# Output projection and FFN turned over, and part of the output sums started inside the sparse attention

## The chip, the cores and the metric

One Trainium2 chip, one of its cores. The metric is the device time of one execution in microseconds (us), the median over several executions. Engines by the profile's names: PE (TensorE), PEld (its weight loads), DVE (VectorE), ACT (ScalarE), POOL (GpSimd), SP (SyncE, which issues all DMAs here).

## The reference, cut to what matters

One layer: three groups of attention heads (gated DeltaNet, dilated, native sparse = NSA) give `mix`, and then

```python
mix = jnp.concatenate([o_dn, o_dil, o_nsa], axis=-1)        # (512, 2048)
x = x + jnp.einsum('bsm,md->bsd', mix, w_out[l])             # output projection, 2048 x 2048
h = rmsnorm(x, norm2_g[l])                                   # x / rms(x) * g
u = causal_dwconv(jnp.einsum('bsd,df->bsf', h, ffn_up[l]), ffn_conv[l])   # 2048 -> 2 x 5632, width 3
u_gate, u_val = jnp.split(u, 2, axis=-1)
x = x + jnp.einsum('bsf,fd->bsd', jax.nn.silu(u_gate) * u_val, ffn_down[l])
return rmsnorm(x, final_g)
```

512 tokens, width 2048 (16 tiles of 128), all in float32.

## The kernel before, in words

**Products.** Every large product of two float32 operands is made of three float32r products: each operand is split into a high part (rounded to float32r) and a low part (the rest), and hi x hi, hi x lo and lo x hi are summed in one PSUM bank. So each step is 3 matmuls of 128x512. The weights come as one long stream in DRAM, in units of 1 MB, a unit being 4 "quarters" of 128 x 512. SP loads a unit into `w_raw` (2 units; `load_unit` L147, which waits until the unit before the last is split), ACT copies each quarter to `w_hi` (`split_hi` L174), DVE subtracts to get `w_lo` (`split_lo` L183), both in a ring of 8 quarters. ACT may split a quarter once PE has used the one 8 before it; at a stage's start 4 quarters are ahead (`AHEAD`). `project` (L222) takes one of 16 steps of a tile with the weights stationary and `h_hi`/`h_lo` (the activations, features on partitions) moving: the result has features on partitions.

**Stages.** DeltaNet, dilated attention, NSA's K/V and compression, then NSA in three rounds `r` = 0, 1, 2 (last), each with two heads (groups g = 0, 1) and four `attend_pe`/`attend_dve`/`attend_act` sequences of 4 query blocks. In rounds 0 and 1 PE's gaps are filled with steps of the next round's q projections (`fill`, counts per block); in the last round there is no fill, and DVE and ACT use their gaps to split 14 of the 16 `mix` tiles (`mix_step`), which SP has loaded back from the DRAM scratch `mix_d` into `h_lo`. The last two heads' outputs are stored too (L1339) and loaded back at the start of the next stage.

**Output projection** (L1503 to L1568): here `h` is stationary and the weights move (L1529), so the result has tokens on partitions and can be added to `xs` (x by tokens, 4 MB, loaded at L1512 between the first two weight units of the stage). 4 column groups of 16 quarters, 12 matmuls to a quarter. **Norm** (`normalize`, L247 to L314): sum of squares and root by ACT, scaling by DVE (L290), 64 transposes on PE (L310), split by ACT (L278) and DVE (L300) into `h_hi`/`h_lo`.

**FFN.** 11 groups of 4 hidden tiles. `up_pe` makes 8 products of 16 steps (`project`, banks 0 to 3); ACT and DVE apply the convolution (L1640, L1664, L1666), SiLU (L1643), the product (L1671) and the split into `g_hi` (L1645) and `g_lo` (L1673). `down_pe` (L1624) has `g` stationary and the weights moving, 4 column groups of 4 quarters in banks 4 to 7, which DVE adds into `xs` (L1686). `g` has two slots, and PE does up(i+1) before down(i). The end: squares and scaling by rows on ACT, DVE and POOL (L1728, L1746, L1735, L1770, L1771), then four DMAs of 1 MB (L1696).

**Places.** By the order of the declarations, a partition's SBUF holds `h_hi` at 0 to 32 KB, `h_lo` to 64, `w_raw` to 80, `w_hi` to 96, `w_lo` to 112, constants and small tiles to about 125, `xs` to about 157, a gain row to about 165, and in the FFN `g_hi` to about 181 and `g_lo` to about 197.

A stage is an `nc.Block`: all engines meet at its end before the next begins.

## Time and profile before

| | us |
|---|---|
| median of 3 runs | 2756.88 |
| lowest and highest run | 2753.33, 2757.06 |
| the profiled execution | 2752.52 |
| its span, first to last instruction | 2750.4 |

The page gives busy time by engine and the granted PE clock by slices; the chain of waits in order of time says which engine the end depends on; the table of stretches gives busy time and clock by stage; the timeline gives start and duration of single instructions. A matmul's duration on the page includes the time in which the next one already runs, so the pace of PE is read from starts, or from a stretch divided by its count.

### The profile page before, as it was taken

The page shows a single profiled execution, that of the slowest core. Times are in us where ns is not written, and L with a number is a line of the kernel's source. Part 1 is how long each engine was busy: PE and PEld are TensorE (multiplying, and loading weights), DVE is VectorE, ACT ScalarE, POOL GpSimd, SP SyncE. Part 2 cuts the span into 40 slices and gives each one's busy share as a digit, 9 for nine tenths or more (in the row PEclk, how much of TensorE's full clock was granted, in tenths as well). Part 3 has the DMA queues.
Part 4 walks back from the last instruction along what each step waited for, and adds up shares of the span by engine and source line. Part 5 has one row for each costly group of instructions (what it writes and reads, how often), then busy time and mean ns, then how long its engine had stood idle before and what let it go on. Part 6 is the DMA issues. An engine that isn't in the chain of part 4 may idle for free.

```text
span 2750.4 us, 33487 instructions
## 1 busy us (share of the span) xinstructions
PE 2603.5 (95%) x11940; PEld 2108.6 (77%) x11940; DVE 1325.3 (48%) x2205; ACT 862.2 (31%) x1601; POOL 72.9 (3%) x54
## 2 busy tenths in 40 slices
PE   7899999989999877998999999999999999999997
PEld 5777877767887544886888888888888888888886
DVE  4776666633344554334444444444444444444444
ACT  4333332332224433224332322232323232322223
POOL 0111011100000000000000000000000000000002
PEclk9999999999999987998999999999999999999999
DMA  4311111131325112422223222222222222223222
GB/s 157 138 59 37 65 65 50 35 115 62 122 92 193 39 61 95 150 92 79 92 92 107 92 97 104 92 92 93 92 102 98 107 94 92 92 93 108 92 92 92
DMA packets 41621, 255.94 MB, mean 93 GB/s; under 512 B 5088, under 2 KB 5344, under 8 KB 13068
## 3 DMA queue, kind: packets, MB, share of 16 engines
q1 hardware_dynamic: 41484, 254.09, 25.8%
q8 instruction: 89, 1.46, 0.2%
q14 instruction: 48, 0.39, 0.0%
HBM read 245.65 MB, written 13.67 MB: 94 GB/s over the span
## 4 chain that ended last, share of the span: by engine, by line
PE 53%; DVE 0%; ACT 0%; issue 0%; DVEq 0%; ACTq 0%
PE bank L222 35%; PE bank L1624 18%; ACT fin_squares L1728 0%; DVE xs L1771 0%; DVE xs L1770 0%; DVE xs L1686 0%; DVEq L1589 0%; ACT fin_rs L1731 0%; ACT L1731 0%; DVE fin_rs L1765 0%; ACTq L1727 0%; DVEq L1750 0%
## 5 line engine op out<-in xcount | busy, mean ns | idle before, releaser
L222 PE MATMUL bank<-h_hi,w_hi 128*128 128x512 f32 x2272 | 919.2, 405 | 29.9 <-DVE w_lo L183 27.3
L222 PE MATMUL bank<-h_lo,w_hi 128*128 128x512 f32 x2272 | 889.8, 392 | 0.0
L222 PE MATMUL bank<-h_hi,w_lo 128*128 128x512 f32 x2272 | 889.5, 392 | 0.0
L183 DVE TENSOR_TENSOR w_lo<-w_raw,w_hi 128x512 fp32r<-128x512 f32 x840 | 555.1, 708 | 420.6 <-ACT w_hi L174 419.1
L174 ACT ACTIVATE w_hi<-w_raw 128x512 fp32r<-128x512 f32 x836 | 488.7, 624 | 721.0 <-PE bank L1624 311.4
L222 PEld LDWEIGHTS bank<-h_hi,w_hi 128*128 128x128 f32 x2272 | 430.0, 189 | 125.4 <-DVE w_lo L183 19.4
L222 PEld LDWEIGHTS bank<-h_lo,w_hi 128*128 128x128 f32 x2272 | 429.2, 189 | 91.9
L222 PEld LDWEIGHTS bank<-h_hi,w_lo 128*128 128x128 f32 x2272 | 430.1, 189 | 87.7 <-issue 4.4
L1624 PE MATMUL bank<-w_hi,g_hi 128*128 128x512 f32 x704 | 277.9, 395 | 0.0
L1624 PE MATMUL bank<-w_lo,g_hi 128*128 128x512 f32 x704 | 277.8, 395 | 0.0
L1624 PE MATMUL bank<-w_hi,g_lo 128*128 128x512 f32 x704 | 277.8, 395 | 0.0
L1686 DVE TENSOR_TENSOR xs<-xs,bank 128x512 f32<-128x512 f32 x176 | 120.9, 687 | 225.8 <-PE bank L1624 220.3
L1664 DVE SCALAR_TENSOR_TENSOR ffn_val<-bank,ffn_wg,ffn_val 128x511 f32<-128x511 f32 x44 | 33.0, 750 | 387.3 <-ACT ffn_val L1640 387.3
L1640 ACT ACTIVATE ffn_val<-bank,ffn_wg 128x512 f32<-128x512 f32 x44 | 30.3, 688 | 424.2 <-PE bank L222 424.2
L1624 PEld LDWEIGHTS bank<-w_hi,g_lo 128*128 128x128 f32 x704 | 132.7, 188 | 30.9
L1624 PEld LDWEIGHTS bank<-w_lo,g_hi 128*128 128x128 f32 x704 | 132.6, 188 | 31.0
L1624 PEld LDWEIGHTS bank<-w_hi,g_hi 128*128 128x128 f32 x704 | 132.6, 188 | 31.0
L1529 PE MATMUL bank<-w_hi,h_hi 128*128 128x512 f32 x256 | 100.3, 392 | 2.0 <-DVEq L1552 2.0
L1529 PE MATMUL bank<-w_lo,h_hi 128*128 128x512 f32 x256 | 100.1, 391 | 0.0
L1529 PE MATMUL bank<-w_hi,h_lo 128*128 128x512 f32 x256 | 100.1, 391 | 0.0
L1746 POOL TENSOR_TENSOR xs<-xs,gain_row 128x512 f32<-128x512 f32 x12 | 16.4, 1418 | 2200.3 <-ACT fin_squares L1728 2200.3
L755 ACT ACTIVATE dn_Y<-bank 128x512 f32<-128x512 f32 x36 | 21.6, 599 | 152.1 <-PE bank L636 152.1
(281 smaller groups left out, 1988.7 us busy)
## 6 DMA issues: line engine op xcount, KB each, us to landing
w_raw<-in_weights SPq DMA_DIRECT2D x209, 1024.0 KB, 4.8
bias_rows<-bias_row SPq DMA_DIRECT2D x10, 512.0 KB, 7.3
mix_scratch<-head_out SPq DMA_DIRECT2D x16, 256.0 KB
xs<-in_x SPq DMA_DIRECT2D x1, 4096.0 KB, 14.6
out<-xs SPq DMA_DIRECT2D x4, 1024.0 KB, 6.1
x_t<-in_x_t SPq DMA_DIRECT2D x3, 1024.0 KB, 11.3
nsa_tab<-bias_rows SPq DMA_DIRECT2D x6, 448.0 KB, 7.2
h_lo<-mix_scratch SPq DMA_DIRECT2D x1, 2560.0 KB, 9.9
```

What stands on the lines that cost most here:

```text
L174: nc.scalar.activation(w_hi[:, act_q.n % RING, :], raw_quarter(act_q), ACT.Copy)\
L183: nc.vector.tensor_tensor(w_lo[:, s, :], raw_quarter(dve_q), w_hi[:, s, :].bitcast(F32), ALU.subtract).then_inc(lo_done, 1)
L222: m = nc.tensor.matmul(PB[pb][:], a[:, s, k], b[:, kt, :], start=(kt == 0 and n == 0), stop=(kt == KT - 1 and n == 2))
L755: nc.scalar.activation(B["Y"][:], W[1][:], ACT.Copy).then_inc(y_a, 1)
L1529: m = nc.tensor.matmul(bank[4 * c + b][:], x[:, kt, b * P:(b + 1) * P], w[:, s, :], start=(kt == 0 and n == 0), stop=(kt == KT - 1 and n = ...
L1624: m = nc.tensor.matmul(W[b][:], x[:, slot, kt, b * P:(b + 1) * P], w[:, s, :], start=(kt == 0 and n == 0), stop=(kt == GT - 1 and n == 2))
L1640: nc.scalar.activation(dst[:], PB[2 * (j % 2) + v][:], ACT.Copy, scale=fwg[:, v, 2, j:j + 1])\
L1664: link(dve, nc.vector.scalar_tensor_tensor(dst[:, 1:SEQ], bk[:, 0:SEQ - 1], fwg[:, v, 1, j:j + 1], dst[:, 1:SEQ], ALU.mult, ALU.add))
L1686: nc.vector.tensor_tensor(dst, dst, W[b][:], ALU.add).then_inc(dn_free, 1)
L1746: nc.gpsimd.tensor_tensor(xs[:, b, cc], xs[:, b, cc], fg[:, cc], ALU.mult).then_inc(fin_g, 1)
```

## The change

- `project` takes its moving operand from a list of tiles on request. The output projection uses `project`: weights stationary, `h` moving, 16 tiles of output features in banks 0 to 3, weights streamed by columns. The FFN's `down_pe` has the weights stationary and `g` moving.
- `x1` (features on partitions, loaded in four DMAs of 1 MB at the start of the stage) takes the place of `xs`. The norm is no stage of its own: squares are summed over tiles in `ssq` (`square`, `add_square`) as the tiles come, the unnormed `x1 * g2` is split (`h2_high`, `h2_low`), a ones-matmul sums `ssq` over partitions, and every `up` result is multiplied by 1/rms (`r2`) on DVE on its way out of PSUM.
- Places: `g_hi`, `g_lo` lie in the first four tiles of `h_hi`, `h_lo`, in one slot. The first four tiles of the FFN's input lie in `near`, the former `w_raw`; from unit 78 (`FFN_UNIT`) the raw weights go to `w_raw_far`, behind `x1`.
- Order: up(i), down(i), with one slot of `g`.
- In NSA's last round 16 steps (48 matmuls; 8 steps of each of output tiles 0 and 1) fill PE's gaps (`WO_FILLS`); their 4 quarters are the ones already split ahead. SP loads one more unit, which ACT and DVE split at the round's end, before DVE's last two copies. The last two heads are split straight from `ob`; no store, no load.
- The end: squares per tile, `ssq`, ones-matmul, root, reciprocal of 128x512, 16 scalings on DVE, eight DMAs of 512 KB.

```diff
+FFN_UNIT = 4 * DN_H + 3 * DIL_H + 6 * NSA_G + 2 * 4 + NSA_H + KT
...
+        near_at = nc.sbuf_base
         w_raw = sb(ctx, "w_raw", [P, 2, 4 * QW])
+        near = nc.alloc_sbuf_tensor_at("near", [P, 2 * GT, SEQ], F32R, offset=near_at)
...
+            hi, lo = (h_hi[:, kt, :], h_lo[:, kt, :]) if tiles is None else tiles[kt]
+            for n, (a, b) in enumerate(((w_hi, hi), (w_lo, hi), (w_hi, lo))):
+                m = nc.tensor.matmul(PB[pb][:], a[:, s, k], b,
...
+        WO_PAIR = [(u, kt) for q in range(4) for u in range(2) for kt in range(4 * q, 4 * q + 4)]
...
+            WO_FILLS = (0, 0, 0, 0), (0, 0, 0, 2), (2, 2, 2, 2), (2, 2, 2, KT)
+            def wo_filler(pe):
+                steps = iter(WO_PAIR[:len(WO_PAIR) // 2])
+                def fill(n):
+                    for u, kt in islice(steps, n):
+                        pe.wait_ge(m_lo, kt + 1)
+                        project(pe, u, kt)
+                return fill
...
             def nsa_dve(dve, r, last):
-                left = [0 if last else 8]
+                left = [4 if last else 8]
...
                 if last:
                     for _ in range(TB):
                         mix_step(mix_lo, dve)
+                    sp_lo(8)
...
-                    load_units(sp, (Q_HEAD + 8 * min(r + 1, NSA_R - 1) + AHEAD + 3) // 4)
+                    load_units(sp, (Q_HEAD + 8 * min(r + 1, NSA_R - 1) + AHEAD + 3) // 4 + (r == NSA_R - 1))
...
+        def h2_high(act, d):
+            nc.scalar.activation(h2[d][0], x1[:, d, :], ACT.Copy, scale=g2[:, d:d + 1]).then_inc(h2_a, 1)
+        def h2_low(dve, d):
+            dve.wait_ge(h2_a, d + 1)
+            nc.vector.scalar_tensor_tensor(h2[d][1], x1[:, d, :], g2[:, d:d + 1], h2[d][0].bitcast(F32),
+                                           ALU.mult, ALU.subtract).then_inc(h2_v, 1)
+        def residual(dve, d):
+            dve.wait_ge(q_used, Q5 + (4 * (d + 1) if d else 7))
+            nc.vector.tensor_tensor(x1[:, d, :], x1[:, d, :], PB[d % 4][:], ALU.add).then_inc(wo_free, 1)
+            dve.wait_ge(wo_free, 4 + d + 1)
...
             def _(sp):
-                sp.wait_ge(stored, 16 * KT + STORED2)
-                for kt in MIX_LATE:
-                    load_mix(sp, [kt], m_in[2])
+                for c in range(CG):
+                    sp.dma_start(x1[:, 4 * c:4 * c + 4, :], t["x_t"][:, 4 * c:4 * c + 4, :]).then_inc(xr_in, 16)
+                sp.dma_start(g2[:], t["g2"]).then_inc(g2_in, 16)
+                sp.dma_start(fg[:], t["final_g"]).then_inc(g2_in, 16)
+                load_units(sp, FFN_UNIT)
                 load_unit(sp)
...
+                for u, kt in WO_PAIR[len(WO_PAIR) // 2:]:
+                    pe.wait_ge(m_lo, len(MIX_EARLY) if kt < MIX_LATE[0] else KT)
+                    project(pe, u, kt)
+                for d in range(2, KT):
+                    pe.wait_ge(wo_free, d + 1)
+                    for kt in range(KT):
+                        project(pe, d % 4, kt)
...
+                dve.wait_ge(xr_in, 64)
+                dve.wait_ge(g2_in, 32)
+                for d in range(KT):
+                    split_lo(dve, 4 if d else 0)
+                    if d < KT - 1:
+                        residual(dve, d)
+                        add_square(dve, d)
+                for d in range(H2A):
+                    h2_low(dve, d)
...
-            g_hi = sb(c7, "g_hi", [P, 2, GT, SEQ], F32R)
-            g_lo = sb(c7, "g_lo", [P, 2, GT, SEQ], F32R)
+            g_hi, g_lo = h_hi[:, 0:GT, :], h_lo[:, 0:GT, :]
...
-                            for n, (x, w) in enumerate(((g_hi, w_hi), (g_lo, w_hi), (g_hi, w_lo))):
-                                m = nc.tensor.matmul(W[b][:], x[:, slot, kt, b * P:(b + 1) * P], w[:, s, :],
+                            for n, (w, x) in enumerate(((w_hi, g_hi), (w_lo, g_hi), (w_hi, g_lo))):
+                                m = nc.tensor.matmul(W[b][:], w[:, s, b * P:(b + 1) * P], x[:, kt, :],
...
+                        nc.vector.tensor_tensor(us[v], PB[2 * (j % 2) + v][:], r2[:], ALU.mult).then_inc(up_free, 1)
...
+                        if last and (c or b):
+                            square_sum(dve, 4 * c + b - 1)
...
+                up_pe(pe, 0, True)
+                with repeat(pe, N_GROUP - 1, (pe_q, GQ, "ffn_pe quarters")) as i:
+                    down_pe(pe, i)
+                    up_pe(pe, i + 1)
+                down_pe(pe, N_GROUP - 1)
+                pe.wait_ge(fin_ss, KT)
+                pe.wait_ge(dn_free, 4 + 16 * N_GROUP)
+                nc.tensor.matmul(W[0][:], ones, ssq[:], start=True, stop=True).then_inc(fin_ps, 1)
...
+                residual(dve, KT - 1)
+                dve.sem_inc(up_free, 1)
+                for d in range(H2A, KT):
+                    h2_low(dve, d)
+                add_square(dve, KT - 1)
...
+                square_sum(dve, KT - 1)
+                dve.wait_ge(fin_root, 1)
+                nc.vector.reciprocal(r2[:], r2[:]).then_inc(fin_ok, 1)
+                dve.wait_ge(fin_ok, 1)
+                for d in range(KT):
+                    nc.vector.scalar_tensor_tensor(x1[:, d, :], x1[:, d, :], fg[:, d:d + 1], r2[:], ALU.mult, ALU.mult)\
+                        .then_inc(fin_v, 1)
```

## Rows read from the trace of the kernel before

**Rows 1.** The page: busy time and share; granted PE clock in 40 slices, tenths.

```profile
PE 2603.5 (95%) x11940; PEld 2108.6 (77%) x11940; DVE 1325.3 (48%) x2205; ACT 862.2 (31%) x1601; POOL 72.9 (3%) x54
...
PEclk9999999999999987998999999999999999999999
```

**Rows 2.** The chain of waits in order of time: start, duration, what.

```profile
1459.31 44.63 PE bank L1624 x192
1503.94 87.06 PE bank L222 x384
```

**Rows 3.** Stretches: length, busy PE, PEld, DVE, ACT, POOL, clock, DMA share, GB/s.

```profile
1048.30:1062.40 14.10, 9.16 (x27) 5.23 (x26) 8.56 (x20) 6.22 (x18) 0.00 (x0) 0.74 0.00 0
...
1082.90:1258.40 175.50, 175.46 (x768) 145.03 (x768) 53.47 (x81) 46.71 (x74) 0.00 (x0) 0.99 0.35 130
1258.40:1285.00 26.60, 14.20 (x66) 12.30 (x65) 22.41 (x39) 14.58 (x29) 0.00 (x0) 0.68 0.00 1
...
1503.60:1590.70 87.10, 87.10 (x386) 72.14 (x385) 36.08 (x60) 24.19 (x42) 0.00 (x0) 1.00 0.28 97
```

**Rows 4.** Timeline of PE, NSA rounds 1 and 2: start, duration, operation [idle before].

```profile
973.39 0.33 PE L972 MATMUL bank<-cst,nsa_lg 128*128 128x128 f32 x1 [1.18 <-DVE nsa_lg L1004]
...
983.07 2.32 PE L986 MATMUL bank<-nsa_PT,nsa_v 128*128 128x512 f32 x8
986.42 0.33 PE L972 MATMUL bank<-cst,nsa_lg 128*128 128x128 f32 x1 [1.02 <-DVE nsa_lg L1004]
...
1052.22 0.27 PE L972 MATMUL bank<-cst,nsa_lg 128*128 128x128 f32 x1
...
1066.10 0.27 PE L972 MATMUL bank<-cst,nsa_lg 128*128 128x128 f32 x1
...
1076.33 4.63 PE L986 MATMUL bank<-nsa_PT,nsa_v 128*128 128x512 f32 x8 [0.69 <-ACT nsa_PT L1023]
```

**Rows 5.** Timeline of PE where the output projection begins.

```profile
1082.94 0.79 PE L1529 MATMUL bank<-w_hi,h_hi 128*128 128x512 f32 x1 [1.98 <-DVEq L1552]
1083.53 0.63 PE L1529 MATMUL bank<-w_hi,h_lo 128*128 128x512 f32 x1
1083.96 0.63 PE L1529 MATMUL bank<-w_lo,h_hi 128*128 128x512 f32 x1
```

**Rows 6.** Timeline of DVE at the end of NSA's last round.

```profile
1081.00 0.69 DVE L1318 COPY head_out<-bank 128x512 f32<-128x512 f32 x1 [2.28 <-PE bank L986]
```

**Rows 7.** Timelines of SP and of ACT in the output projection's first 20 us.

```profile
1084.60 1.31 SPq L147 DMA_DIRECT2D w_raw<-in_weights  x1
1085.95 0.43 SPq L1512 DMA_DIRECT2D xs<-in_x  x1
...
1090.79 2.20 ACT L174 ACTIVATE w_hi<-w_raw 128x512 fp32r<-128x512 f32 x4 [1.91 <-DMA w_raw<-in_weights]
1103.19 2.20 ACT L174 ACTIVATE w_hi<-w_raw 128x512 fp32r<-128x512 f32 x4 [10.20 <-DMA w_raw<-in_weights]
```

**Rows 8.** Timeline of DVE in the norm.

```profile
1262.67 2.74 DVE L290 SCALAR_TENSOR_TENSOR n_y<-xs,n_rs,gain_row 128x512 f32<-128x512 f32 x4
```

**Rows 9.** Timeline of PE, a compression product (two f32 matmuls in two passes each).

```profile
892.83 1.98 PE L1211 MATMUL bank<-cmp_PT,v_cmp 31*128 31x512 f32 x4
```

**Rows 10.** Timelines of ACT and DVE after an FFN up product.

```profile
1591.03 0.69 ACT L1640 ACTIVATE ffn_val<-bank,ffn_wg 128x512 f32<-128x512 f32 x1 [9.68 <-PE bank L222]
...
1591.83 0.75 DVE L1664 SCALAR_TENSOR_TENSOR ffn_val<-bank,ffn_wg,ffn_val 128x511 f32<-128x511 f32 x1 [8.88 <-ACT ffn_val L1640]
...
1594.94 0.69 DVE L1673 TENSOR_TENSOR g_lo<-ffn_prod,g_hi 128x512 fp32r<-128x512 f32 x1 [0.70 <-ACT g_hi L1645]
```

**Rows 11.** Groups by line: count, busy us, mean ns, idle before.

```profile
L183 DVE TENSOR_TENSOR w_lo<-w_raw,w_hi 128x512 fp32r<-128x512 f32 x840 | 555.1, 708 | 420.6 <-ACT w_hi L174 419.1
L174 ACT ACTIVATE w_hi<-w_raw 128x512 fp32r<-128x512 f32 x836 | 488.7, 624 | 721.0 <-PE bank L1624 311.4
...
L791 DVE RECIPROCAL dn_A<-dn_A 128x512 f32<-128x512 f32 x6 | 20.1, 3353 | 3.3 <-ACT dn_A L740 3.0
```

**Rows 12.** Timelines of DVE, PE, ACT and SP at the end.

```profile
2731.67 3.06 DVE L1686 TENSOR_TENSOR xs<-xs,bank 128x512 f32<-128x512 f32 x4 [8.10 <-PE bank L1624]
2733.33 0.40 PE L1624 MATMUL bank<-w_lo,g_hi 128*128 128x512 f32 x1
2735.58 1.28 ACT L1731 ACT_TABLE_LOAD   x1
...
2738.64 3.91 SPq L1696 DMA_DIRECT2D out<-xs  x4
```

More of the change, by code:

```diff
@@ L1199, in nsa_pe @@
                     m.then_inc(c_s, 1)
-                fill(8)
+                fill(0 if last else 8)
                 for g in range(NSA_G):
@@ L1267, in nsa_dve @@
             def nsa_dve(dve, r, last):
-                left = [0 if last else 8]
+                left = [4 if last else 8]
                 def sp_lo(k):
@@ L1862, in down @@
             rows(ffn_down, g * GT * P, c)
-    up(0)
-    for g in range(1, N_GROUP):
+    for g in range(N_GROUP):
         up(g)
-        down(g - 1)
-    down(N_GROUP - 1)
+        down(g)
     return np.stack(units)
```

402 lines of the change are left out of this document (155 added, 247 removed).

## The prediction

> **What bounds the kernel now.** I read first the busy shares and the clock by slices, then the chain of waits in order of time, then the stretches by stage, and single instructions at the seams last. PE is busy 95% of the span, at full clock but for three slices in the attention [rows 1]. In the FFN the chain is PE alone: one piece of 384 up matmuls and one of 192 down matmuls, eleven times over, with nothing between them [rows 2]. So work taken from DVE or ACT there is worth nothing, and only three things can move the end: the pace of PE's matmuls, the places where PE stands idle, and the tail after its last matmul. The idle places that this change touches are the last NSA round, where PE is busy 9.16 us of 14.1 at a mean clock of 0.74, and the norm, a stretch of 26.6 us with 64 small transposes; the output projection between them is dense: 768 matmuls in 175.5 us [rows 3].
>
> All sums below are against the profiled execution: span 2750.4 us, device time 2752.5. The median of the runs shown, 2756.9, is 4.4 us above it, and I add the change to the median at the end.
>
> **Step 1, the pace of the down projection.** Up: 87.06 us / 384 = 226.7 ns a matmul. Down: 44.63 / 192 = 232.4 ns [rows 2]. The output projection of before has the very loop shape of down (activations stationary, weights moving, a bank for every three matmuls) and takes (175.5 - 1.4)/768 = 226.7 ns [rows 3], the 1.4 us being its slow start (step 3). So neither which operand is stationary nor the banks cost anything; what is left as different is the place of `g`, above 165 KB, while all operands of the other two lie below 112 KB. The change puts `g` below 48 KB and leaves every operand of every large product below 112 KB, `near` included. I take 226.7 for down: 2112 x 5.7 ns = **-12.0 us**, all of it on the chain. Bounds: 0, if the place isn't the cause, and -12. In the Trainium skill, "TensorE: Matmul & The Clock Gate", section "Back-to-back issue gap", a warm matmul of 512 columns takes 518 cycles, about 216 ns, and nothing is said of where in SBUF its operands lie. By that rule moving them gains nothing, which is rival A; the trace agrees with neither its figure nor its silence, as it has two paces for one shape.
>
> **Step 2, the norm.** Of the 26.6 us [rows 3] nothing stays. In its place:
> - The meeting at the stage's end. At the last such seam DVE's last instruction ended at 1081.69 [rows 6] and PE began at 1082.94 [rows 5], 1.25 us later. Now PE itself ends last and DVE is done; I take 0.9 us, bound 1.3.
> - The first up product needs `h2` tile by tile. Tiles 0 to 3 (`near`) are ready before, 12 matmuls = 2.7 us of cover. The others wait for the residual of tile 15 (0.7), ACT (0.7) and DVE (0.75), so tile 4 comes some 2.9 us after the end against PE's 0.9 + 2.7 = 3.6; from there DVE makes one per 0.66 us (four in 2.74, [rows 8]) and PE eats one per 0.68. No stall, with little to spare: 0, bound 3.
> - The ones-matmul in full float32: two passes of about 0.43 (four in 1.98 us, [rows 9]): 0.9 us.
> - DVE then adds the last square, copies the conv taps and splits quarter 5 of the FFN while PE wants it: 0.3, bound 2.
>
> The root and the 3.35 us reciprocal [rows 11] run beside two or more products of 10.9 us, for which banks are free. Sum -26.6 + 0.9 + 0.9 + 0.3 = **-24.5 us**, bounds -26 and -20.
>
> **Step 3, the last NSA round and the output projection.** The 48 matmuls put into the round take 10.9 us of PE time there. They fit: in round 1 an attend with 7 fill steps takes 986.42 - 973.39 = 13.0 us, in the last round without any 1066.10 - 1052.22 = 13.9 [rows 4]; the pace is DVE's. The last PV product ran at half clock, 4.63 us against 2.32 [rows 4]; with PE busier it may gain up to 2.3. But at the round's end DVE now splits 4 quarters (4 x 0.71 [rows 11] = 2.8 us) before its two copies, which before waited 2.28 us for PE [rows 6]. The one takes back most of the other: PE begins the next stage 0.5 us earlier, bounds 3 earlier and 3 later.
>
> There 720 matmuls are left, 163.2 us. A start at half clock costs 1.4 us as it does now (7 matmuls at 0.43 instead of 0.23 [rows 5]). The new thing is the queue on SP. Now a unit of weights is issued first, then the 4 MB of x, then the next unit. In the new order x goes first, all 4 MB, then two small loads, and behind them the unit with the quarters after the first eight. ACT began on the first unit 4.9 us after its issue ended (1084.60 + 1.31), and 4 + 1 MB more took till 1103.19, that is 2.48 us a MB [rows 7]. So from the stage's start at about 1081.9: 0.7 for the first issue, 4.9 + 4 x 2.48 = 14.8 for x and the unit, 1.0 for the small loads (0 to 4; the trace has nothing of their size behind a full queue), 0.62 + 0.71 [rows 11] to split the first quarter: 1099.7. Who waits for it: DVE and ACT, which also wait for x and the gains before they take any split of the stage, and PE, whose 48 prepared matmuls carry it to 1082.4 + 10.9 + 1.4 = 1094.7. PE stalls 5.0 us and pays about 1.4 more for the half clock after it. Sum 163.2 + 1.4 + 5.0 + 1.4 = 171.0 against 175.5: -4.5, with the start -**5.0 us**, bounds -12 (no stall) and +4.
>
> **Step 4, the FFN's order.** With one slot, down(i) needs the g of its own up(i). It takes its quarters in order, so the last hidden tile is wanted 3 x 12 x 0.227 = 8.2 us after up's end. The chain now runs from 1591.03 to 1595.63, 4.6 us [rows 10]; the product with `r2` puts one DVE operation of 0.7 and a wait before it: 5.4. Cover 8.2, so **0**. Behind this chain on DVE stand the splits of the next quarters, wanted 10.9 us after; 5.4 + 0.7 is in time. DVE gains 88 products of 0.7 us = 60 us in all, in stretches where it is more than half idle (36.1 busy in 87.1 [rows 3]). Loads, x twice before and twice now: 0.
>
> **Step 5, the tail.** Now it is 2750.4 - 2733.73 = 16.7 us [rows 12]. New, from PE's last end T: DVE must do adds and square sums in turn for the last four tiles, nine operations of some 0.75 (four adds with waits take 3.06 [rows 12]) from T-1.85: T+4.9. Ones-matmul at half clock, as PE is idle: 1.9, T+6.9. Root on ACT 0.7 (its table load, 1.28 [rows 12], fits beside the matmul): T+7.6. Reciprocal 3.35 [rows 11]: T+11.0. Sixteen scalings at 0.66 [rows 8]: T+21.7. The last 512 KB: I take 4.0 for issue, transfer and landing, under the 4.9 of a 1 MB load [rows 7], as DVE's pace of 1.33 us per 512 KB is no faster than the queue's 1.24; the meeting 0.4. T+26.1, **+9.4 us**, bounds +6 and +12. Nothing hides it.
>
> **Sum**: -12.0 - 24.5 - 5.0 + 0 + 9.4 = **-32.1 us**: 2720.4 in terms of the profiled execution, 2724.8 in terms of the median.
>
> **Rivals.**
> - **A, the pace of down stays.** The 5.7 ns come from something else than `g`'s place. For: no row shows one operand in two places. Against: the output projection, same shape, at 226.7. Sum -20.1: 2736.8.
> - **B, the x load costs more.** Smaller pieces or the gains' loads hold the queue, or the filled last round is slowed by its steps as well: 10 us more than step 3. For: the only stage in which PE has but 11 us of stock against 16 us of queue. Against: the 4 MB ran at full rate before. -22: 2735.
> - **C, the single slot of g turns the FFN into stop and go, slower than before.** Place: the fourth tile of each down. If DVE doesn't take up the chain at once at up's end, since splits stand before it in program order, all 11 seams stall. The kernel becomes slower once each stalls more than (32.1 + 5.5)/11 = 3.4 us, so when the chain takes over 11.6 us instead of 5.4; with nothing covered it would be 11 x 5.4 = 59 us, +27: 2784. Against: at up's end in the trace ACT takes the bank at once and DVE follows 0.1 us after ACT [rows 10], its splits done by then.
> - **D, PE's end moves but the tail and the x load eat it**: rival A with the upper bounds of steps 2, 3 and 5: -20.1 + 4.5 + 9.0 + 2.6 = -4.0: 2752.9. For: all four are independent of each other and open. Against: it needs all of them.
>
> **How the numbers follow.** Forecast (all steps within their bounds, down at 226.7) 64%; A 14%; B 14%; C 4%; D 4%. The likeliest is the forecast, 2724.8. The range runs to A and B on the upper side, 2741 with the bound of the tail, and on the lower side to no stall in step 3, 2714. Faster by over 0.2% (5.5 us, about what a measurement of this kernel can tell from no change): forecast, A, B and a quarter of D, 93%; within 0.2%: half of D, 2%; slower: C and the rest of D, 5%.
>
> **What would show it.** Right: in the chain of waits the down pieces of 192 are 43.5 us long, and no wait of PE on `h_lo`/`g_lo` stands between the pieces; between the output projection and the first up piece there are under 4 us; PE waits some 5 us on `w_lo`, whose chain goes back to a weights DMA, some 11 us into the output projection; the stretch after the last FFN matmul is 26 us. Wrong: down pieces of 44.6 us (A); a gap of PE in front of the fourth quarter of each down (C); a wait on x or the weights of 10 us and more (B); fill matmuls after which the attention's transposes come later than 14 us apart (step 3).

## The result and the profile after

| | before | after |
|---|---|---|
| median | 2755.15 us | 2722.11 us |
| lowest and highest run | 2753.33, 2757.06 | 2718.94, 2723.40 |
| the profiled execution, and its span | 2752.5, 2750.4 | 2723.4, 2721.6 |

The ratio of after to before is 0.9878, with a 95% interval of 0.9861 to 0.9895: 33.0 us less, where 32.1 less had been predicted (2724.8 us, range 2714 to 2741, from the 2756.9 us of the first three runs; the median of before is now one of four). The number was right. Of its reason for the faster down projection, the second largest term, that can't be said: the runs below show another cause than the one predicted.

The page of the kernel after, busy time of PE and DVE and the granted PE clock in 40 slices, to be laid beside [rows 1]:

```profile
PE 2581.6 (95%) x11880; PEld 2098.2 (77%) x11880; DVE 1398.9 (51%) x2313; ACT 859.5 (32%) x1578; POOL 55.7 (2%) x42
...
PEclk9999999999999997999999999999999999999998
```

PE has 60 instructions and 21.9 us of work less: the 64 small transposes of the norm are gone, four passes of ones-matmuls came. One low slice of the clock is left where there were three, and a new one stands at the very end. The chain of waits in order of time (start, duration, what), for [rows 2]:

```profile
1256.78 11.17 PE bank L231 x48
1267.95 0.86 PE bank L1575 x2
1268.81 76.19 PE bank L231 x336
1345.00 43.52 PE bank L1588 x192
1388.52 87.04 PE bank L231 x384
```

From the first FFN product on PE has no gap. Line 231 is `project`, 1575 the ones-matmul of the norm, 1588 the down projection: 43.52 us for 192 matmuls, 226.7 ns each, where [rows 2] has 44.63. Next the stretches by stage (length, busy PE, PEld, DVE, ACT, POOL with their counts, clock, DMA share, GB/s), for [rows 3]; in order they are the output projection, the first FFN product with its seam, a down and an up piece, the last down group, and what follows PE's last FFN product:

```profile
1085.80:1256.60 170.80, 168.06 (x720) 138.22 (x720) 61.25 (x97) 44.35 (x81) 0.00 (x0) 0.97 0.32 117
1256.60:1268.30 11.70, 11.52 (x51) 9.38 (x51) 10.65 (x22) 10.75 (x19) 0.00 (x0) 1.00 0.52 191
1345.00:1388.50 43.50, 43.50 (x194) 36.03 (x193) 23.28 (x36) 13.22 (x22) 0.00 (x0) 1.00 0.28 97
1388.50:1475.50 87.00, 87.00 (x386) 72.06 (x385) 40.40 (x67) 24.88 (x42) 0.00 (x0) 1.00 0.27 97
2650.60:2696.50 45.90, 44.88 (x192) 35.30 (x191) 27.48 (x43) 16.33 (x28) 0.00 (x0) 1.00 0.07 23
2696.50:2721.60 25.10, 2.08 (x2) 0.50 (x2) 18.00 (x23) 3.87 (x6) 0.00 (x0) 0.56 0.42 167
```

The timeline of PE at both ends of the last attention round (start, duration, operation, [idle before]): the round's first product, its last PV product, the output projection's first matmul, and the first one after its only stall, for [rows 4, 5]:

```profile
1016.26 0.97 PE L1157 MATMUL bank<-k_cmp,nsa_q 128*128 128x31 f32 x7
...
1079.77 2.42 PE L923 MATMUL bank<-nsa_PT,nsa_v 128*128 128x512 f32 x8 [0.69 <-ACT nsa_PT L960]
...
1085.85 0.77 PE L231 MATMUL bank<-h_hi,w_hi 128*128 128x512 f32 x1 [3.66 <-PEq L1096]
...
1102.19 0.76 PE L231 MATMUL bank<-h_hi,w_hi 128*128 128x512 f32 x1 [2.39 <-DVE w_lo L191]
```

And of the kernel before, the round's first product:

```profile
1011.34 0.85 PE L1197 MATMUL bank<-k_cmp,nsa_q 128*128 128x31 f32 x6
```

With these the spans can be laid side by side, 2750.4 against 2721.6, -28.8 us:

| stretch | before | after | difference | predicted |
|---|---|---|---|---|
| start to the last round's first product | 1011.3 | 1016.3 | +4.9 | 0 |
| from there to the output projection's first matmul | 71.6 | 69.6 | -2.0 (see below) | -0.5 |
| output projection | 175.5 | 170.3 | -5.2 | -4.5 |
| norm and seam | 26.6 | 1.5 | -25.1 | -24.5 |
| eleven down pieces at their pace | | | -12.2 | -12.0 |
| stalls in the last down group | 0 | 2.4 | +2.4 | 0 |
| after PE's last FFN product | 16.7 | 25.1 | +8.4 | +9.4 |

The first line isn't the change's. The code up to there is the same in all kernels of this study, but for the places of tiles in three of them, and in the profiled executions that stretch ended anywhere from 1009.7 to 1016.3 us. Part of it shows in the stretch 944 to 976 us, where attention products begin (kernel before, after, and e4_tail below, in this order): the clock is 0.89, 0.84 and 1.00 there.

```profile
944.00:976.00 32.00, 26.46 (x105) 16.68 (x104) 17.11 (x55) 11.84 (x40) 0.00 (x0) 0.89 0.22 82
```

```profile
944.00:976.00 32.00, 27.49 (x105) 17.56 (x104) 14.41 (x46) 12.15 (x36) 0.00 (x0) 0.84 0.21 82
```

```profile
944.00:976.00 32.00, 25.86 (x114) 16.96 (x113) 18.24 (x57) 13.61 (x43) 0.00 (x0) 1.00 0.22 82
```

The second line scatters too, over less: in the profiled executions of nine further kernels whose last round is that of the kernel after, it reads 69.6 (e9_unit_tail) to 71.0 us (e7_g_mid), so between -0.6 and -2.0 against the one execution of before. So single profiles are compared below by stages, and whole kernels by medians. Without that line the change is worth -33.7 us by its stages. (The 1.5 us of the norm are 0.63 between the last product of the output projection and the first of the FFN, and the 0.86 of the ones-matmul.)

### The profile page after: what moved, and what is told of

It reads as the page before. It is cut to its first block, busy times and chain, and to the rows that moved or that the text cites. A ratio compares the mean times of both kernels' runs of the same rounds, so it can differ in the third digit from the quotient of the medians.

```text
span 2721.6 us, 33363 instructions
## 1 busy us (share of the span) xinstructions
PE 2581.6 (95%) x11880; PEld 2098.2 (77%) x11880; DVE 1398.9 (51%) x2313; ACT 859.5 (32%) x1578; POOL 55.7 (2%) x42
## 4 chain that ended last, share of the span: by engine, by line
PE 53%; DVE 1%; ACT 0%; issue 0%; DVEq 0%; ACTq 0%
PE bank L231 35%; PE bank L1588 17%; DVE x_t L1737 0%; DVE head_out L1668 0%; ACT head_out L1711 0%; DVE rms_row L1734 0%; PE bank L1690 0%; DVE x_t L1660 0%; PE bank L1575 0%; ACT rms_row L1713 0%; DVEq L1550 0%; ACTq L1710 0%; DVEq L1717 0%
## 5 line engine op out<-in xcount | busy, mean ns | idle before, releaser
L231 PE MATMUL bank<-h_hi,w_hi 128*128 128x512 f32 x2176 | 887.5, 408 | 36.9 <-DVE w_lo L191 32.0
L231 PE MATMUL bank<-h_lo,w_hi 128*128 128x512 f32 x2176 | 855.4, 393 | 0.0
L231 PE MATMUL bank<-h_hi,w_lo 128*128 128x512 f32 x2176 | 854.9, 393 | 0.0
L182 ACT ACTIVATE w_hi<-w_raw_far 128x512 fp32r<-128x512 f32 x528 | 307.1, 624 | 439.4 <-PE bank L1588 274.8
L191 DVE TENSOR_TENSOR w_lo<-w_raw_far,w_hi 128x512 fp32r<-128x512 f32 x528 | 331.2, 687 | 123.8 <-ACT w_hi L182 122.5
L191 DVE TENSOR_TENSOR w_lo<-w_raw,w_hi 128x512 fp32r<-128x512 f32 x312 | 215.8, 735 | 202.8 <-ACT w_hi L182 202.5
L1588 PE MATMUL bank<-h_hi,w_hi 128*128 128x512 f32 x704 | 274.4, 390 | 1.0 <-DVE x_t L1660 1.0
L1588 PE MATMUL bank<-h_hi,w_lo 128*128 128x512 f32 x704 | 273.9, 389 | 0.0
L1588 PE MATMUL bank<-h_lo,w_hi 128*128 128x512 f32 x704 | 273.9, 389 | 0.0
L231 PE MATMUL bank<-near,w_hi 128*128 128x512 f32 x704 | 231.5, 390 | 0.5 <-DVEq L1717 0.5
L182 ACT ACTIVATE w_hi<-w_raw 128x512 fp32r<-128x512 f32 x308 | 176.8, 621 | 94.4 <-DMA w_raw<-in_weights 48.7
L231 PEld LDWEIGHTS bank<-near,w_hi 128*128 128x128 f32 x704 | 132.1, 188 | 28.4 <-DVEq L1717 0.9
L231 PE MATMUL bank<-near,w_lo 128*128 128x512 f32 x352 | 136.9, 389 | 0.0
```

The source lines that it names most:

```text
L182: nc.scalar.activation(w_hi[:, act_q.n % RING, :], raw_quarter(act_q), ACT.Copy)\
L191: nc.vector.tensor_tensor(w_lo[:, s, :], raw_quarter(dve_q), w_hi[:, s, :].bitcast(F32), ALU.subtract).then_inc(lo_done, 1)
L231: m = nc.tensor.matmul(PB[pb][:], a[:, s, k], b, start=(kt == 0 and n == 0), stop=(kt == KT - 1 and n == 2))
L1588: m = nc.tensor.matmul(W[b][:], w[:, s, b * P:(b + 1) * P], x[:, kt, :], start=(kt == 0 and n == 0), stop=(kt == GT - 1 and n == 2))
```

## Experiments

All are edits of the kernel after, and differences are against its 2722.11 us. The kernel before was measured beside each group of them and had medians of 2755.1 to 2757.0 us, so a difference of 2 us between medians of different groups says little.

### What makes the down projection faster

The first question was whether `g`'s place does it. In the built programs the first tile starts at 16.1 KB (byte 16512), so all addresses are some 16 KB above the places that stand ahead of the prediction: `g` was at 181.5 to 213.5 KB, and the operands of all fast products of the kernels before and after lie below 128.2 KB. e1_g_high puts `g` alone back up:

```diff
-            g_hi, g_lo = h_hi[:, 0:GT, :], h_lo[:, 0:GT, :]
+            g_hi, g_lo = (sb(c7, n, [P, GT, SEQ], F32R) for n in ("g_hi", "g_lo"))
```

> The changed kernel with g_hi and g_lo, and nothing else, put back at the upper end of SBUF (two tiles of 8 KB behind all others, at about 179 to 195 KB) in place of the first four tiles of h_hi and h_lo. Theory (the place of the moving operand sets PE's pace): the down pieces of 192 matmuls in the chain of waits go back from 43.5 to 44.6 us, 232.4 ns a matmul, up pieces stay at 87.0; 2112 x 5.7 ns = +12.0 us against the changed kernel. Rival (the pace of before came from g being the stationary operand there, or from its two slots): down stays at 43.5 and the time is that of the changed kernel within 2 us.

Measured 2734.94 us (2733.47 to 2737.33), +12.8, and in the chain of e1_g_high:

```profile
1387.39 87.07 PE bank L231 x384
1474.46 44.80 PE bank L1588 x192
```

Up stays, down takes 44.80 us, 233.3 ns a matmul. So it is where `g` lies, moving or stationary. e5_w_hi_far moves the other operand, in the FFN only, up:

```diff
+            hi_far.append(sb(c7, "w_hi_far", [P, RING, QW], F32R)[:])
...
+            wh = hi_of(pe_q.n)
-            for n, (a, b) in enumerate(((w_hi, hi), (w_lo, hi), (w_hi, lo))):
+            for n, (a, b) in enumerate(((wh, hi), (w_lo, hi), (wh, lo))):
```

> The changed kernel with the ring of w_hi, from the FFN's first quarters on, in a new tile at the upper end of SBUF (about 182 to 198 KB); w_lo and all moving operands stay low. So the stationary operand of two of every three matmuls of the FFN, up and down, lies high. Theory in its wide form (any matmul operand high in SBUF slows PE, as each of the three did when g lay there): the pace goes from 226.7 to 232.4 ns for two thirds or for all of the FFN's 6336 matmuls, +24 to +36 us. Theory in its narrow form (in the kernel before it was the weight load of g, hidden or not, that differed; or only the moving operand counts): no difference, up pieces 87.0 and down pieces 43.5 us.

Measured 2749.23 us (2744.68 to 2751.45), +27.1: 6336 matmuls by (231.1 - 226.7) ns are 27.9. Chain of e5_w_hi_far:

```profile
1388.56 88.75 PE bank L237 x384
1477.31 44.37 PE bank L1596 x192
```

So the stationary operand counts too, and in up as in down: the wide form of the theory. Up to here everything fits the predicted reason, "high is slow". e7_g_mid looks for the border, and takes one possible confusion away (the tiles' start within 64 bytes); e8_pad tests that one by itself; e11_border lays the ring of `w_hi` over the range next to 128 KB:

```diff
+        sb(c5, "pad_mid", [P, 8])
+        g_hi, g_lo = (sb(c5, n, [P, GT, SEQ], F32R) for n in ("g_hi", "g_lo"))
         x1 = sb(c5, "x1_t", [P, KT, SEQ])
```

> The changed kernel with g_hi and g_lo in front of x1 and not behind everything: by the allocator's addresses, which begin with the first tile at 16 KB, at 141.5 to 157.5 KB (in e1_g_high 189.6 to 205.6 KB, in the kernel before 181.5 to 213.5, the operands of all fast products below 128.2 KB). Start on a multiple of 64 bytes, as the tiles of the fast products have and those of e1_g_high and e5_w_hi_far had not. Theory (height: a border lies somewhere between 128 and 181 KB): either 43.5 or 44.6 us for a down piece, which tells on which side of 141.5 KB the border is; I expect 44.6 us, +12 us, since 128 KB is the nearest round number. Rival (a gradual cost, or one of the distance between the two operands): a value between 43.5 and 44.6 us.

```diff
+        sb(ctx, "pad_first", [P, 8])
         h_hi = sb(ctx, "h_hi", [P, KT, SEQ], F32R)
```

> The changed kernel with 32 bytes of padding in front of the first tile, so that all operands of the large products start 32 bytes past a multiple of 64 bytes, as g in e1_g_high and w_hi in e5_w_hi_far did; nothing else moves. Theory (height alone sets the pace): up 87.0 and down 43.5 us, the time of the changed kernel. Rival (the start within 64 bytes sets it, wholly or in part): all large products slower, up to 233 ns instead of 226.7; over 10,000 such matmuls up to +60 us.

```diff
+        cst = sb(ctx, "cst", [P, N_CST, P])
+        eps_t = sb(ctx, "eps_t", [P, 1])
+        one_t = sb(ctx, "one_t", [P, 1])
+        ob = [sb(ctx, f"head_out{g}", [P, SEQ]) for g in range(NSA_G)]
+        sb(ctx, "pad", [P, 7])
         h_hi = sb(ctx, "h_hi", [P, KT, SEQ], F32R)
...
+        w_lo = sb(ctx, "w_lo", [P, RING, QW], F32R)
         w_hi = sb(ctx, "w_hi", [P, RING, QW], F32R)
-        w_lo = sb(ctx, "w_lo", [P, RING, QW], F32R)
-        cst = sb(ctx, "cst", [P, N_CST, P])
...
```

> The changed kernel with its constants and two small tiles declared first and the rings of w_lo and w_hi in the other order, so that by the allocator's addresses the eight slots of w_hi begin at 122.7, 124.7, 126.7, ... 136.7 KB; all other operands of the large products lie below 122.7 KB. Theory (a border in height between 128.2 KB, below which all fast products lie, and 141.5 KB, where e7_g_mid was slow, at 128 KB as the round number): the FFN's steps whose quarter lies in slots 0 and 1 keep 226.7 ns, those of slots 3 to 7 take some 231 ns as in e5_w_hi_far, slot 2, which lies across 128 KB, is in between; about +30 us over the kernel's large products. Rival (the border is higher, or the cost belongs to other tiles than the weights' ring at such a height): all slots at 226.7 ns, or the step elsewhere between two slots.

Measured: e7_g_mid 2734.94 us (+12.8, as expected), e8_pad 2720.38 (2719.34 to 2722.2, unchanged, as expected), e11_border 2720.98 (two runs; +30 had been expected, and nothing came). One down piece of each, in this order:

```profile
1473.17 44.79 PE bank L1589 x192
```

```profile
1474.37 43.52 PE bank L1589 x192
```

```profile
1473.10 43.52 PE bank L1589 x192
```

e8_pad rules out the start within 64 bytes. The other two leave a theory of height only an odd place for its border, between 138.7 KB (the end of the fast ring of e11_border) and 141.5 KB (where `g` of e7_g_mid starts; down is slow there from its first matmuls on). With the addresses of all kernels, as the built programs hold them, side by side another pattern stands out. In a partition one tile of an operand (512 values) is 2048 bytes, and the operands' starts modulo 2048 are:

| kernel | h, near | w_hi, w_lo | g | pace of down, ns |
|---|---|---|---|---|
| before | 128 | 128 | 1536 | 232.4 |
| after | 128 | 128 | 128 | 226.7 |
| e1_g_high | 128 | 128 | 1632 | 233.3 |
| e7_g_mid | 128 | 128 | 1536 | 233.3 |
| e5_w_hi_far | 128 | w_hi 736, w_lo 128 | 128 | 231.1 |
| e8_pad | 160 | 160 | 160 | 226.7 |
| e11_border | 736 | 736 | 736 | 226.7 |

e12_phase sets the two theories against each other in one kernel: `g` high but on the offset of the weights, and `h` low but off it.

```diff
-        near_at = nc.sbuf_base
+        cst, tok = sb(ctx, "cst", [P, N_CST, P]), sb(ctx, "tok", [P, DN_H, 5, TB])
+        sb(ctx, "pad_w", [P, 104])
+        w_at = near_at = nc.sbuf_base
...
-        cst = sb(ctx, "cst", [P, N_CST, P])
...
-        tok = sb(ctx, "tok", [P, DN_H, 5, TB])
...
-            g_hi, g_lo = h_hi[:, 0:GT, :], h_lo[:, 0:GT, :]
+            sb(c7, "pad_g", [P, (w_at - nc.sbuf_base) % 2048 // 4])
+            g_hi, g_lo = (sb(c7, n, [P, GT, SEQ], F32R) for n in ("g_hi", "g_lo"))
```

> The changed kernel with two places changed. A constant tile and padding stand between h_lo and w_raw, so that w_raw (near), w_hi and w_lo start 1536 bytes past a multiple of 2048 while h_hi and h_lo start 128 past one; all of them stay below the 138.7 KB up to which e11_border was fast. And g_hi and g_lo lie high, at 191.5 to 207.5 KB, on 1536 past a multiple of 2048, as the weights do. In every kernel so far the fast products had both operands on the same offset modulo 2048 (128 and 128, in e8_pad 160 and 160, in e11_border 736 and 736) and the slow ones had not (1536 or 1632 against 128, in e5_w_hi_far 736 against 128). Theory of height (a border between 138.7 and 141.5 KB): up pieces stay at 87.0 us, down pieces go to 44.8; +13 us, 2735. Theory of the offset (operands on different offsets in 2048 bytes slow each other down, wherever they lie): the other way round, down pieces stay at 43.5 us, high as g lies; of an up product the first 12 of 48 matmuls (near, same offset as the weights) stay at 226.7 ns and the other 36 take 231 to 233, so up pieces of 88.3 to 89.0 us, and all large products ahead of the FFN are slow as well; with some 3170 of the FFN's 4224 up matmuls, 720 of the output projection and the attention's on the path, +25 to +40 us, 2747 to 2762.

Measured 2747.8 us (2745.72 to 2752.78), +25.7. Chain of e12_phase, and PE's timeline inside one up product, from its first matmul with `near` to some with `h`:

```profile
1393.21 89.00 PE bank L232 x384
1482.21 43.54 PE bank L1589 x192
```

```profile
1404.16 0.39 PE L232 MATMUL bank<-near,w_hi 128*128 128x512 f32 x1
...
1406.89 0.40 PE L232 MATMUL bank<-h_hi,w_hi 128*128 128x512 f32 x1
...
1408.29 0.40 PE L232 MATMUL bank<-h_hi,w_hi 128*128 128x512 f32 x1
```

The other way round from height, as the theory of the offset says: down, with `g` at 191.5 KB, runs at 226.8 ns, and up, all of it below 138.7 KB, is slow. Inside a product the 12 matmuls on `near`, which shares the weights' offset, take 2.73 us, 227.5 ns each, and the next six, on `h`, 1.40 us, 233 ns each. Of the 25.7 us, 21.6 are the eleven up pieces (89.0 against 87.04) and 3.6 the output projection (174.5 against 170.9, up to the first FFN product), which has `h` off the weights too; the last attention round began at 1014.4 us, within the scatter of the others, so from the products ahead of it nothing is seen in the time. What is shown: operands that start on the same offset modulo 2048 bytes run at 226.7 ns a matmul wherever they lie, and at 231.1 to 233.3 ns with the three differences tried (608, 1408 and 1504 bytes). The modulus itself must be smaller. The stationary operand is a quarter of its tile, 512 bytes a partition, so in the kernel after its start differs from the moving one's by 0, 512, 1024 or 1536 bytes in turn, and all four are fast. So at most the offset modulo 512 counts; modulo 128 isn't enough, since 1408 is 11 x 128 and slow. 512 or 256 is left open. And in e5_w_hi_far the third matmul, on `w_lo` and `h_hi`, both at 128, had the slow pace as well; the load of the next matmul's `w_hi` runs beside it, but that this is the reason was not tried by itself. Why an offset costs time at all is open.

### What the filling of the last round is worth

```diff
-            WO_FILLS = (0, 0, 0, 0), (0, 0, 0, 2), (2, 2, 2, 2), (2, 2, 2, KT)
+            WO_FILLS = ((0, 0, 0, 0),) * 4
...
-                for u, kt in WO_PAIR[len(WO_PAIR) // 2:]:
+                for u, kt in WO_PAIR:
```

> The changed kernel without the 48 matmuls in the last NSA round; they are done at the start of the output projection. Theory (the fill takes up time in which PE is idle anyway, and its clock is low there): 48 x 0.227 = 10.9 us come into the output projection, which in return loses the stall of 2.5 us on the weights behind the x load and the half clock after it of 1.5, since PE now has 96 matmuls in stock; and the round's last product of PV runs at half clock again, 2 us: +8 to +9 us against the changed kernel. Rival (the last round is bound by DVE and ACT, to which the fill adds, so that without it the round ends earlier by as much as the fill is worth): within 3 us of the changed kernel.

Measured 2726.56 us (2723.8 to 2727.7), +4.5: between the two theories, and neither's number. Timeline of PE (e2_no_fill), the last PV product and the output projection's start, then the stretch of the output projection:

```profile
1078.27 4.63 PE L923 MATMUL bank<-nsa_PT,nsa_v 128*128 128x512 f32 x8 [0.69 <-ACT nsa_PT L960]
1084.35 0.47 PE L231 MATMUL bank<-h_hi,w_hi 128*128 128x512 f32 x1 [1.45 <-PEq L1096]
```

```profile
1084.30:1259.20 174.90, 174.50 (x768) 143.99 (x768) 61.12 (x97) 44.34 (x81) 0.00 (x0) 1.00 0.31 115
```

PE does 48 matmuls more here, 10.9 us, but the stage is only 4.6 longer than after's 170.3. At 226.7 ns each the 768 would take 174.1, so next to nothing is lost; of after's 170.3, 7.1 us are loss (720 x 0.2267 = 163.2). The fill emptied PE's stock of 96 matmuls to 48 ahead of a queue that delivers the next weights at a fixed time, and left the clock low behind the seam. The round itself costs the same with and without fill: the last PV product takes 4.63 us at half clock instead of 2.42, and PE goes on at the same point, 6.08 us after that product's start in both (and 69.5 us after the round's first product, against 69.6), because DVE, not PE, ends the round.

### The stall on the weights behind x

```diff
             def _(sp):
+                load_unit(sp)
                 for c in range(CG):
                     sp.dma_start(x1[:, 4 * c:4 * c + 4, :], t["x_t"][:, 4 * c:4 * c + 4, :]).then_inc(xr_in, 16)
...
-                dve.wait_ge(xr_in, 64)
-                dve.wait_ge(g2_in, 32)
                 for d in range(KT):
-                    split_lo(dve, 4 if d else 0)
+                    split_lo(dve, 4 if d < KT - 1 else 0)
+                    if d == 0:
+                        dve.wait_ge(xr_in, 64)
+                        dve.wait_ge(g2_in, 32)
```

(ACT's splits are moved in the same way.)

> The changed kernel with one unit of weights issued ahead of the four x loads at the output projection's start, and ACT and DVE splitting its four quarters before they wait for the gains and x. Theory (PE's stall of 2.5 us comes from the weights queued behind 4 MB of x): the stall at some 13 us into the stage is gone, with the half clock after it of 1.5 us; the first residual waits for x some 2.5 us longer, which four banks cover: -4 us against the changed kernel. Rival (the x load is then what PE waits for, through the residual that frees its bank): the stall comes later and as long, no difference.

Measured 2716.59 us (2715.95 to 2717.45), -5.5 for the expected -4. The stretch of e3_unit_first's output projection:

```profile
1084.00:1248.60 164.60, 164.53 (x720) 136.06 (x720) 64.23 (x97) 49.82 (x81) 0.00 (x0) 0.99 0.33 122
```

PE is busy throughout; 170.3 has become 164.5, 1.3 above the 163.2 of full pace. The stall and all but the first half-clock stretch are gone, and nothing comes later in their place, as the rival had it. The first half-clock stretch differs by itself from one execution to the next: it lasts some seven matmuls here and some thirteen in e9_unit_tail, which has the same edit, behind the same 3.66 us of idle time; there the stage takes 166.3 us. So 5.5 is at the upper end of what the edit brings.

### The end

```diff
                         nc.vector.tensor_tensor(dst, dst, W[b][:], ALU.add).then_inc(dn_free, 1)
-                        if last and (c or b):
-                            square_sum(dve, 4 * c + b - 1)
+                    for b in range(4 if last and c < CG - 1 else 0):
+                        square_sum(dve, 4 * c + b)
...
-                nc.tensor.matmul(W[0][:], ones, ssq[:], start=True, stop=True).then_inc(fin_ps, 1)
+                nc.tensor.matmul(W[0][:], ones, ssq[:], start=True, stop=False)
+                for i, s4 in enumerate((sq[:], us[0], us[1], gf)):
+                    pe.wait_ge(fin_sq, KT - 4 + i + 1)
+                    m = nc.tensor.matmul(W[0][:], ones, s4, start=False, stop=(i == 3))
```

> The changed kernel with another order at its end: in the last down group DVE adds all four tiles of a column group before it sums their squares, and the squares of the last four tiles are not summed on DVE but go to four tiles of their own, which the ones-matmul sums in PSUM in five steps. Theory (DVE's square sums stand between PE and its banks in the last group, 2.4 us, and 5.1 us of DVE stand between PE's last product and the ones-matmul): the gaps of 0.4 and 0.9 us in the last down piece go (-2.4 us), the ones-matmul starts some 2 us after PE's end instead of 5.1 but takes five matmuls instead of one, so the root comes 0 to 2 us sooner; together -2.5 to -4.5 us against the changed kernel. Rival (ACT's squares, not DVE's sums, are what ends last): -2.4 us from the gaps, and a tail as long or longer, -2.4 to 0.

Measured 2715.43 us (2712.49 to 2719.88), -6.7. Chain of e4_tail:

```profile
2645.43 43.52 PE bank L1588 x192
2688.95 0.86 PE bank L1690 x2
2689.80 3.45 PE bank L1693 x8
```

The last down piece is 43.52 us long again (-2.4), and 22.15 us follow instead of 25.1 (-3.0): -5.4 by the stages, a little more than the expected 2.5 to 4.5. The ones-matmul begins at PE's end and not 2 us later, and without a pause before them all its passes run at full clock (granted 1.00), ten in 4.3 us, where the kernel after takes 2.08 us for two.

e6_all adds e3_unit_first's edit and shares the last scaling out:

```diff
+                for d in range(KT - 4, KT):
+                    nc.scalar.activation(x1[:, d, :], x1[:, d, :], ACT.Copy, scale=fg[:, d:d + 1]).then_inc(fin_g, 1)
...
+                for d in range(KT - 4, KT):
+                    nc.gpsimd.tensor_tensor(x1[:, d, :], x1[:, d, :], r2[:], ALU.mult).then_inc(fin_p, 1)
```

> The changed kernel with the two edits of e3_unit_first and e4_tail, and the final scaling shared out: ACT multiplies the last four tiles by the gain while the root is being taken, POOL multiplies them by 1/rms while DVE scales the other twelve; the 512 KB pieces go out in the order in which they are ready. Theory: the gains add, since they lie at different places of the chain: -5.5 (e3_unit_first measured), -2.5 to -4.5 (e4_tail's expectation), and 4 x 0.66 = 2.6 us of DVE's 10.7 us of scaling less, if POOL's four products, which no trace here shows, stay under DVE's 8 us: -10 to -12 us against the changed kernel. Rival (POOL and DVE slow each other down, or the DMA of 4 MB is what bounds the last 10 us, at 1.24 us per 512 KB): no more than -8 us.

Measured 2713.39 us (2712.65 to 2714.37), -8.7, short of the expected -10 to -12. Timelines of DVE and POOL of e6_all while the output is scaled, and the two stretches with and without POOL at work (columns as above):

```profile
2692.94 12.15 DVE L1746 SCALAR_TENSOR_TENSOR x_t<-x_t,fin_g,rms_row 128x512 f32<-128x512 f32 x12
```

```profile
2692.99 6.26 POOL L1754 TENSOR_TENSOR x_t<-x_t,rms_row 128x512 f32<-128x512 f32 x4 [2178.64 <-DVE rms_row L1743]
```

```profile
2692.90:2699.25 6.35, 0.00 (x0) 0.00 (x0) 6.32 (x5) 0.00 (x0) 6.26 (x4) 0.50 0.21 83
2699.25:2705.10 5.85, 0.00 (x0) 0.00 (x0) 5.84 (x9) 0.00 (x0) 0.00 (x0) 0.50 0.77 307
```

DVE needs 12.15 us for twelve scalings; the kernel after did sixteen in 10.69. While POOL works on four of its own, DVE gets through between three and four in 6.3 us (the first takes 1.85); the others, behind POOL's end, take 5.84 us at the old pace of 0.67 each, with more DMA beside them. So DVE is held up by more than the four were worth. e9_unit_tail is e6_all without that part:

```diff
-                for d in range(KT - 4):
+                for d in range(KT):
                     nc.vector.scalar_tensor_tensor(x1[:, d, :], x1[:, d, :], fg[:, d:d + 1], r2[:], ALU.mult, ALU.mult)
...
-                for d in (0, 2, 4, 12, 6, 8, 14, 10):
+                for d in range(0, KT, 2):
```

> The changed kernel with the two edits of e3_unit_first and e4_tail and nothing else (e6_all without the shared scaling). Theory (the two gains add, and in e6_all it was the shared scaling that cost 4.1 us in the tail, 26.2 us instead of 22.1): -5.5 and -5.5 against the changed kernel, so about 2711, with a stretch of 22.1 us after the last product of the FFN. Rival (the gain of the tail's edit in e4_tail came in part from an earlier arrival of the attention, which is chance): -8, 2714, the same as e6_all.

Measured 2712.3 us (2707.57 to 2713.05), -9.8. The stretch after the last FFN product, e6_all and then e9_unit_tail:

```profile
2684.50:2710.70 26.20, 4.30 (x11) 1.55 (x9) 16.47 (x15) 5.82 (x9) 6.26 (x4) 0.66 0.40 160
```

```profile
2689.00:2711.20 22.20, 4.29 (x11) 1.55 (x9) 15.01 (x19) 3.38 (x5) 0.00 (x0) 0.71 0.48 189
```

The shared scaling cost 4.0 us there. Of these 1.5 are DVE's (12.15 us against 10.69 for all sixteen). The other 2.5 stand behind its last scaling, which ends 5.6 us before the end instead of 3.1: the finished tiles come late and bunched, and the output DMAs, 512 KB each, land 3.8 us after their issue (median) instead of 2.7. So both halves of the rival expected for e6_all took part. The medians of the two kernels differ by 1.1 only, and e9_unit_tail's lies between the two forecasts. In the profiled executions the 4.0 us are hidden by what comes before: e9_unit_tail's last round began 4.3 us later and was 1.2 shorter, and its output projection took 1.4 us more, for a longer stretch at half clock at its start. Between the rivals the tail decides, and it speaks for the theory.

### The seam before the output projection

```diff
                         mix_step(mix_lo, dve)
-                    sp_lo(8)
+                    sp_lo(1)
...
                 dve.sem_inc(wo_free, 4)
+                split_lo(dve, 1)
                 for i in range(len(MIX_EARLY), KT):
                     mix_lo(dve, i)
+                split_lo(dve, 2)
```

> e9_unit_tail with three of DVE's four weight splits at the end of the last NSA round moved behind the stage's seam, where PE needs one only every 2.7 us. Theory (PE's 3.66 us of idle time between its last PV product and the output projection are DVE's: four splits of 0.70 stand ahead of the two copies that end the round): the idle time falls by 3 x 0.70 = 2.1 us to 1.6, and as in e2_no_fill, where it was 1.5, the clock is then still full when PE goes on, 1.4 us more: -2 to -3.5 us against e9_unit_tail. Rival (ACT's four splits or the meeting of the engines hold the seam as long): no difference.

Measured 2705.25 us (2703.33 to 2708.54), ratio to the kernel before 0.9819 (0.9805 to 0.9833), -7.1 against e9_unit_tail, where -2 to -3.5 had been expected. PE's timeline:

```profile
1076.63 2.42 PE L923 MATMUL bank<-nsa_PT,nsa_v 128*128 128x512 f32 x8 [0.69 <-ACT nsa_PT L960]
1080.91 0.47 PE L231 MATMUL bank<-h_hi,w_hi 128*128 128x512 f32 x1 [1.85 <-PEq L1096]
```

The idle time is 1.85 us instead of 3.66, and PE starts at full clock, though it drops to the half for seven matmuls 1.5 us later. From the first matmul of the stage to the ones-matmul of the norm it is 176.7 us against 178.0. Together these are 3.1 us, within the forecast. The two profiled executions differ by 5.2 us, and 2.4 of them lie ahead of the last round, in the stretch that scatters by itself; why the medians differ by 7.1 isn't accounted for. It is the fastest of these kernels.

## Why the prediction was right, and where it wasn't

**Step 1, the pace.** The term was right to 0.2 us (-12.2), its reason wrong. "What is left as different is the place of `g`, above 165 KB" took one difference for the only one: `g` also began on another offset modulo 512 bytes than the weights (0 against 128), and e12_phase shows that this is what counts, and height isn't. That the number came out was luck in so far as the change put `g` into `h`'s tiles, which cures both. The rule "low is fast" would mislead whoever packs tiles low with small ones between them: e12_phase does that, and takes 25.7 us more. Rival A, that nothing changes, would have followed from the Trainium skill, "TensorE: Matmul & The Clock Gate", section "Back-to-back issue gap", with its some 216 ns for a warm matmul of 512 columns by itself. The page has a second figure there, some 131 ns a matmul in a sustained stream, which the prediction left out. The runs show 226.7 ns at best and 233.3 for the same shape, and agree with neither.

**Step 2, the norm.** -25.1 for -24.5. The seam itself is a gap of 0.47 us, and no wait of PE on `h2` follows; the ones-matmul's 0.86 us is the 0.9 of the sum. The 0.3 for DVE's late split did not appear.

**Step 3, the last round and the output projection.** -7.2 for -5.0. The weights behind x came nearly as forecast: PE went on 16.3 us after the stage's first matmul, the prediction's 1099.7 - 1082.4 is 17.3. The start at half clock lasted longer than before, thirteen matmuls instead of seven, but cost nothing: up to the arrival of the weights PE has time to spare, so what the slow start took, the stall (2.4 us of idle time instead of 5.0) gave back. The prediction has these two in the right relation: its stall is what is left after the slow start, and 1.4 + 5.0 is the 17.3 less the 10.9 of stock. So the stage came out at 170.3 us for 171.0: the weights came 1.0 earlier, and the half clock behind the stall cost a little more than its 1.4. What the sum doesn't show is the value of the fill, whose 10.9 us of PE work are taken out of the stage while the stall stands beside them as a cost of the queue: e2_no_fill shows that the fill brought 4.6, the rest being the stall and the half clock that it caused. Of the predicted "0.5 us earlier" the profile has 2.0, but the last rounds of the same code scatter over 1.4 us, so this is no clear miss. The faster PV product was worth nothing there, since its half clock is covered by DVE's work in any case (6.08 us from its start to the next stage with and without the fill); in the kernel before it is 6.61.

**Step 4, the order.** No gap before or inside any middle down piece; the cover of 8.2 us against 5.4 held, and rival C with it fell. But its last group was overlooked: there `square_sum` stands between DVE's adds, and PE waits for `dn_free`. In the waits of the kernel after, from 2650.4 us on:

```profile
PEld bank L1588 <- DVE x_t L1660: 3.0, 5, 0.9
...
PE bank L1690 <- DVE head_out L1668: 5.1, 1, 5.1
```

The first row (waited for in total, times, longest) is the weight loads held up, 3.0 us; on the chain the last down group is 45.9 us long instead of 43.5, the missed +2.4. e4_tail took it away by letting DVE do its four adds before any square sum. The prediction did cost these operations, in step 5, but asked only who waits for them at the end. With the term the forecast would have been 2727.2 us.

**Step 5, the tail.** +8.4 for +9.4. Here the second row above (5.1 us) is the forecast T+4.9; then come the ones-matmul in 2.08 us at half clock, the root, the reciprocal (3.35) and the scalings (10.69). The sum itself, from T+4.9 by its own terms, gives T+25.8 and not T+26.1: rounding added 0.3. The last 512 KB took less than the 4.0 us assumed: in the list of issues (KB each, median us to landing) 2.7.

```profile
out<-x_t SPq DMA_DIRECT2D x8, 512.0 KB, 2.7
```

Rivals B and D did not come about: the stage with the x load lay within 1 us of its forecast. Of rival A the time did not come, but its condition did: the 5.7 ns come from something else than the height of `g`.

## What to carry to other kernels

When one product is slower than another of the same shape, write down the SBUF addresses of both operands and their difference modulo 512 bytes, not only the region that they are in; some bytes of padding decided here. Work moved into an idle stretch is worth its own time only if the stage that it leaves can still run on what is ready: count the stock that it takes away from the front of the next queue. And a new operation on DVE is to be asked twice who waits: for its own result, and for what stands behind it.

## What the runs showed of the hardware that was not expected

- Two float32r operands of 128x512 matmuls whose starts differ modulo 512 bytes (by 96, 384 or 480) cost 231.1 to 233.3 ns a matmul instead of 226.7, whether they lie low or high (e12_phase, e1_g_high, e5_w_hi_far); in the whole kernel, with `h` off the weights' offset, 25.7 us.
- POOL on its own part of the same tile held DVE up: beside four POOL products (6.26 us) DVE got through between three and four scalings, the first in 1.85 us, against 0.67 alone; behind POOL's end it was back at 0.67 (e6_all). How long POOL's products take alone no run here shows.
- The same code ahead of the last attention round took 6.5 us more or less from one execution to the next, and the granted clock in one 32 us stretch of it was 0.84 to 1.00 in the three executions compared.
